# Rows spilled from full expert blocks: from blocks of 96 rows to units of 32 rows

## The reference

```python
g_sel = argmax(x @ w_group + b_group)            # one of 4 groups
top_v, top_i = top_k(le[rows, g_sel], 2)         # two of the 8 experts of that group
gate = softmax(top_v) * pg[rows, g_sel]
h = silu(xr @ w_gate[e]) * (xr @ w_up[e])        # 1024 -> 512
y[token] += gate * (h @ w_down[e])               # 512 -> 1024
```

## Time and profile before

| | us |
|---|---|
| median of three runs (1839.2, 1839.83, 1849.47) | 1839.83 |
| the profiled execution's own time | 1853.84 |
| its span | 1852.1 |
| PE busy (share of the span) | 1759.5 (95%) |
| DVE busy | 747.6 (40%) |
| ACT busy | 326.1 (18%) |
| POOL busy | 196.3 (11%) |
| mean granted TensorE clock | 0.975 |

### The profile page before, as it was taken

One profiled execution on the slowest core, in us unless ns is written; L12 is line 12 of the kernel. 1 busy time (PEld: TensorE's weight loads), 2 busy tenths in 40 slices (PEclk: granted clock), 3 DMA queues, 4 the chain that ended last, 5 costly groups with the idle time before them and its releaser, 6 DMA issues. The chain is left out here.

```text
span 1852.1 us, 34664 instructions
## 1 busy us (share of the span) xinstructions
PE 1759.5 (95%) x15263; PEld 1143.8 (62%) x15263; DVE 747.6 (40%) x1172; ACT 326.1 (18%) x741; POOL 196.3 (11%) x190
## 2 busy tenths in 40 slices
PE   8999999999999999999989999759999999999976
PEld 4565556646666644445666665438777777778742
DVE  1213456515766743400013444554334443344337
ACT  1211224401334210110001111001011110011016
POOL 2100000002322000000000000041111111111103
PEclk9999999999999999999999999779999999999998
DMA  6261011001002041343110001529999999999967
GB/s 212 71 211 46 1 45 50 1 1 49 1 13 91 4 159 34 123 142 114 46 46 12 24 23 68 228 92 406 422 424 418 415 422 419 419 420 413 368 235 276
DMA packets 72887, 322.32 MB, mean 174 GB/s; under 512 B 14481, under 2 KB 29129, under 8 KB 59745
## 3 DMA queue, kind: packets, MB, share of 16 engines
q1 hardware_dynamic: 47856, 280.70, 38.0%
q10 hardware_dynamic: 17360, 22.03, 3.6%
q0 software_dynamic: 7584, 18.38, 2.8%
HBM read 288.05 MB, written 37.65 MB: 176 GB/s over the span
## 5 line engine op out<-in xcount | busy, mean ns | idle before, releaser
L860 PE MATMUL psum<-arena 128*32 128x256 f32 x6144 | 375.0, 381 | 14.3 <-DVE arena L1942 6.3
L860 PEld LDWEIGHTS psum<-arena 128*32 128x32 f32 x6144 | 270.3, 110 | 108.5 <-issue 53.3
L457 PE MATMUL psum<-arena 128*128 128x512 f32 x640 | 282.7, 600 | 3.0 <-issue 3.0
L1466 DVE COPY arena<-psum 128x512 f32<-128x512 f32 (+6 forms) x128 | 83.8, 663 | 369.1 <-PE psum L457 201.3
L457 PEld LDWEIGHTS psum<-arena 128*128 128x128 f32 x640 | 121.8, 193 | 150.5 <-issue 150.1
L869 PE MATMUL psum<-arena 128*32 128x256 f32 x3072 | 180.6, 379 | 0.7 <-DVE arena L1916 0.5
L680 PE MATMUL psum<-arena 128*128 128x352 f32 x576 | 177.9, 460 | 0.0
L442 PE MATMUL psum<-arena 128*128 128x352 f32 x576 | 170.8, 459 | 0.1
L869 PEld LDWEIGHTS psum<-arena 128*32 128x32 f32 x3072 | 139.2, 110 | 31.7 <-issue 1.4
L1174 ACT ACTIVATE arena<-psum 128x128 f32<-128x128 f32 (+7 forms) x193 | 94.1, 497 | 345.0 <-PE psum L435 244.0
L442 PEld LDWEIGHTS psum<-arena 128*128 128x128 f32 x576 | 109.4, 190 | 61.3 <-issue 0.8
(11 more groups left out here) (273 smaller groups left out, 1575.7 us busy)
## 6 DMA issues: line engine op xcount, KB each, us to landing
arena<-in_moe_w_down SPq DMA_DIRECT2D x34, 2048.0 KB, 15.2
arena<-in_moe_w_gate SPq DMA_DIRECT2D x34, 2048.0 KB, 13.2
arena<-in_moe_w_up SPq DMA_DIRECT2D x34, 2048.0 KB, 18.4
y_blocks<-arena ACTq DMA_DIRECT2D x136, 96.0 KB, 12.0
arena<-in_w_in SPq DMA_DIRECT2D x6, 2048.0 KB, 9.9
y_blocks<-arena ACTq DMA_DIRECT2D x1, 8448.0 KB, 45.9
arena<-in_x_prompt SPq DMA_DIRECT2D x9, 512.0 KB, 3.3
arena<-in_w_out SPq DMA_DIRECT2D x2, 2048.0 KB, 7.9
```

The lines of the kernel that those rows point to most:

```text
L457: last = mm(ps[0:n, c * 512:(c + 1) * 512], lhs(k), rhs(k)[:, c * 512:(c + 1) * 512], start=(k == 0), stop=(k == KD - 1))
L860: last = mm(out, xeT[:, b, a, k, :], gu[b][:, :, k, j * P:(j + 1) * P], start=(k == 0), stop=(k == KD - 1))
L1466: take(V.tensor_copy(out, src), key)
```

## The change

Rows of rank 96 and above are now worked in units of 32 rows. A unit has one gather, one gate column and one store of its own; it loads the three weights of its expert as a block did. `NU` = 66 units are possible, and every loop and every list of tests goes to that number. The number of units of an expert is its rows over 96, divided by 32 and rounded up; the units lie one after the other in the same space of `y_blocks`, three to a former block. The table `over_i` is larger (66 units by 32 experts), and it is worked out behind `tables_ready` and the gates, under a semaphore of its own (`over_ready`) for which all engines wait ahead of `n_over`. POOL writes six of the nine tiles of the second choice's `pick`, DVE the other three. A unit's buffer in PSUM is two banks apart from the other's, for gate and up as for down.

```diff
-            link(TS(ovn, cnt, 1.0 / C, -(C / 2 + 0.5) / C, ALU.mult, ALU.add))
+            link(TS(ovn, cnt, 1.0 / 32, 0.5 - 1.0 / 64 - NS, ALU.mult, ALU.add))
...
-            STT(RR, TB_, -float(C), RR, ALU.mult, ALU.add).then_inc(places_ready, 1)
-            link(TS(TA, TB_, 1.0, None, ALU.is_ge))
-            link(TT(OO, OO, TB_, ALU.add))
-            link(STT(OO, OO, float(NE - 1), EE, ALU.add, ALU.subtract))
+            link(STT(RR, TB_, -32.0, RR, ALU.mult, ALU.add))
+            link(TS(TA, TB_, float(NS), None, ALU.is_ge))
+            link(STT(OO, OO, float(NS * NE - NS), EE, ALU.add, ALU.subtract))
             link(TT(OO, OO, TA, ALU.mult))
-            link(TT(EE, EE, OO, ALU.add))
+            link(TT(TB_, EE, TB_, ALU.add))
+            link(TT(TB_, TB_, OO, ALU.add))
+            link(TS(EE, TB_, 1.0 / NS, -1.0 / NS, ALU.mult, ALU.add))
+            link(TS(EE, EE, ROUND, -ROUND, ALU.add, ALU.add))
+            link(STT(OO, EE, -float(NS), TB_, ALU.mult, ALU.add))
+            STT(RR, OO, 32.0, RR, ALU.mult, ALU.add).then_inc(places_ready, 1)
...
+                if k == 1:
+                    for t0, t1 in ((BY_POOL, NT - 1), (NT - 1, NT)):
+                        n, nt = rows_of(t0), t1 - t0
+                        last = TT(pick[0:n, 1, t0:t1, :], row_iota[0:n, :].unsqueeze(1).to_broadcast([n, nt, C]),
+                                  vals[0:n, 6, t0:t1].unsqueeze(2).to_broadcast([n, nt, C]), ALU.is_equal)
...
-            link(TT(over3, oend.unsqueeze(1).to_broadcast([P, NOVER, NE]),
-                    blk_iota[:, 0:NOVER].unsqueeze(2).to_broadcast([P, NOVER, NE]), ALU.is_le))
...
             take(V.tensor_copy(gates, both[:, 1]), ("GT",))
             emptied(dve, ("GT",))
+            link(TT(over3, oend.unsqueeze(1).to_broadcast([P, NU, NE]),
+                    unit_iota.unsqueeze(2).to_broadcast([P, NU, NE]), ALU.is_le))
+            link(V.tensor_reduce(over_f[:, 0:NU], over3, AX.X, ALU.add))
+            link(TS(over_f[:, 0:NU], over_f[:, 0:NU], float(NE - 1), None, ALU.min))
+            link(V.tensor_copy(over_f[:, NU:NU + 1], oend[:, NE - 1:NE]))
+            V.tensor_copy(over_i, over_f).then_inc(over_ready, 1)
```

PE, SP and ACT in `spilled` (DVE has the silu of one tile in place of three):

```diff
-                for a in range(NS):
-                    for k in range(KD):
...
+                for k in range(KD):
+                    for q in range(4):
+                        last = mm(O_U[b][32 * q:32 * q + 32].rearrange("p (m n) -> p m n", m=2), xeT[:, b, 0, k, :],
+                                  gu[b][:, :, k, q * P:(q + 1) * P], start=(k == 0), stop=(k == KD - 1))
+                last.then_inc(o_gu, 1)
...
             with pe.If(n_over > 2):
-                with pe.Fori(1, NOVER // 2) as i:
+                with pe.Fori(1, NU // 2) as i:
...
-                    sp.wait_ge(o_gu, 3 * j - 3)
+                    sp.wait_ge(o_gu, j - 1)
...
-                    sp.wait_ge(o_dn, 2 * j - 2)
+                    sp.wait_ge(o_dn, j - 1)
...
+                act.wait_ge(o_gu, j + 1)
+                A(sg[:, 0, :], O_U[b], ACT.Exp, scale=-1.0).then_inc(g_exp, 1)
                 act.wait_ge(o_gate, j + 1)
-                act.wait_ge(o_dn, 2 * j + 1)
+                act.wait_ge(o_dn, j + 1)
...
+                A(ye[b][:, 0, :], O_Y[b], ACT.Copy, scale=gate2[:, b, 0:1]).then_inc(o_y, 1)
                 act.wait_ge(o_y, j + 1)
-                store_y(y_dram[bass.ds(j * C + NE * C, C), :], b, o_out)
+                for q in range(4):
+                    act.dma_start(y_dram[bass.ds(j * 32 + NE * C, 32), 256 * q:256 * q + 256],
+                                  ye[b][32 * q:32 * q + 32, 0, :]).then_inc(o_out, 16)
                 act.wait_ge(o_out, 64 * j + 64)
                 A(lnv[:, 0:1], eps_ln, ACT.Copy)
...
             with act.If(n_over > 2):
-                with act.Fori(1, NOVER // 2) as i:
+                with act.Fori(1, NU // 2) as i:
...
-            for j in range(NOVER):
+            pool.wait_ge(over_ready, 1)
+            n_over = pool.value_load(over_i[0:1, NU:NU + 1], min_val=0, max_val=NU)
+            for j in range(NU):
                 with pool.If(n_over > j):
...
-                    gather(NE + j, j % 2, [o_x[j % 2]] * NS)
+                    gather_tile(NE + j // NS, j % 2, j % NS, 0, o_x[j % 2])
```

More of the change, by code:

```diff
@@ L30 @@
 NB = NE + NOVER
+NU = NS * NOVER
 ALPHA = 2.0 ** 0.25
@@ L227, in build @@
         assert rt[0] <= R + 17408
+        over3 = view(R + 13312, "j e", j=NU, e=NE)
+        gates_of_unit = gates.rearrange("p n a -> p (n a)")
         g1 = view(0, "t n", t=NT, n=D)
@@ L831, in _ @@
                 for t in range(NT):
-                    if k == 1:
+                    if k == 1 and t < BY_POOL:
                         pe.wait_ge(row_ready, t + 1)
@@ L899, in _ @@
             down(1).then_inc(y_done, 1)
-            pe.wait_ge(tables_ready, 1)
-            n_over = pe.value_load(over_i[0:1, NOVER:NOVER + 1], min_val=0, max_val=NOVER)
-            O_Y = psum[:, 6 * BANK:8 * BANK]
+            pe.wait_ge(over_ready, 1)
+            n_over = pe.value_load(over_i[0:1, NU:NU + 1], min_val=0, max_val=NU)
+            O_U = [psum[:, 2 * b * BANK:2 * b * BANK + 256] for b in range(2)]
+            O_Y = [psum[:, (4 + 2 * b) * BANK:(4 + 2 * b) * BANK + 256] for b in range(2)]
             def spilled(j, b, turn_n):
@@ L911, in spilled @@
                     pe.wait_ge(y_ready, NE - 1 + j)
-                for a in range(NS):
-                    for k in range(KD):
[L914 to L918, removed]
-                pe.wait_ge(o_down[b], 16 * turn_n + 16)
[L920 to L931, removed]
+                for k in range(KD):
[3 more added lines that the diff above has]
+                last.then_inc(o_gu, 1)
+                pe.wait_ge(o_down[b], 16 * turn_n + 16)
+                if not isinstance(j, int):
+                    pe.wait_ge(o_y, j - 1)
+                pe.wait_ge(o_h, j + 1)
+                for k in range(KE):
+                    for q in range(4):
+                        last = mm(O_Y[b][32 * q:32 * q + 32], hhT[:, b, 0, k, :], wd[b][:, k, q * 256:(q + 1) * 256],
+                                  start=(k == 0), stop=(k == KE - 1))
+                last.then_inc(o_dn, 1)
             with pe.If(n_over > 0):
@@ L1125, in _ @@
             load_down(NE - 1, 1, NE - 2)
-            sp.wait_ge(tables_ready, 1)
-            n_over = sp.value_load(over_i[0:1, NOVER:NOVER + 1], min_val=0, max_val=NOVER)
+            sp.wait_ge(over_ready, 1)
+            n_over = sp.value_load(over_i[0:1, NU:NU + 1], min_val=0, max_val=NU)
             def spilled(j, b):
@@ L1148, in _ @@
             with sp.If(n_over > 2):
-                with sp.Fori(1, NOVER // 2) as i:
+                with sp.Fori(1, NU // 2) as i:
                     for b in range(2):
@@ L1404, in _ @@
             y_rows(NE - 1, 1, 3, NE // 4 - 1)
-            act.wait_ge(tables_ready, 1)
-            n_over = act.value_load(over_i[0:1, NOVER:NOVER + 1], min_val=0, max_val=NOVER)
-            O_Y = psum[:, 6 * BANK:8 * BANK]
+            act.wait_ge(over_ready, 1)
+            n_over = act.value_load(over_i[0:1, NU:NU + 1], min_val=0, max_val=NU)
+            O_U = [psum[:, 2 * b * BANK:2 * b * BANK + P] for b in range(2)]
+            O_Y = [psum[:, (4 + 2 * b) * BANK:(4 + 2 * b) * BANK + 256] for b in range(2)]
             def spilled(j, b):
@@ L1798, in _ @@
                     V.memset(place[:, :, NT - 1, :], 0.0)
-                    V.memset(pick[:, 0, NT - 1, :], 0.0)
+                    V.memset(pick[:, :, NT - 1, :], 0.0)
                 if s >= 4:
@@ L1838, in _ @@
             of_chosen(e_iota, EE)
+            link(TS(EE, EE, float(NS), None, ALU.mult))
             rk = filled(dve, ("RK",))
@@ L1950, in _ @@
             dve_expert(NE - 1, 1, NE // 2 - 1, last_one=True)
-            n_over = dve.value_load(over_i[0:1, NOVER:NOVER + 1], min_val=0, max_val=NOVER)
+            dve.wait_ge(over_ready, 1)
+            n_over = dve.value_load(over_i[0:1, NU:NU + 1], min_val=0, max_val=NU)
             def spilled(j, b, turn_n):
-                dve.wait_ge(o_x[b], 16 * NS * turn_n + 16 * NS)
-                turn_x(b).then_inc(o_xt, 1)
+                dve.wait_ge(o_x[b], 16 * turn_n + 16)
+                V.transpose(xeT[:, b, 0], xe[:, b, 0].rearrange("p (d k) -> p k d", k=KD)).then_inc(o_xt, 1)
                 if isinstance(j, int):
@@ L1982, in _ @@
             with dve.If(n_over > 2):
-                with dve.Fori(1, NOVER // 2) as i:
+                with dve.Fori(1, NU // 2) as i:
                     for b in range(2):
@@ L2096, in _ @@
             pool.wait_ge(masks_ready, 1)
-            link(Q.memset(pick[:, 1, NT - 1, :], 0.0))
             pool.wait_ge(places_ready, 1)
-            for t in range(NT):
-                n = rows_of(t)
-                Q.tensor_scalar(pick[0:n, 1, t, :], row_iota[0:n, :], vals[0:n, 6, t:t + 1], None, ALU.is_equal)\
+            for t in range(BY_POOL):
```

(1 more changed line is left out.)

66 lines of the change are left out of this document (28 added, 38 removed).

## The result

The changed kernel takes **1888.09 us** (median of four runs, 1881.43 to 1892.24), the kernel before beside it on the same chip 1844.34: a ratio of **1.024, 95% interval 1.0201 to 1.0278**, slower by some 44 us. The forecast was 1875 us, with a range of 1856 to 1895 and a chance of 0.84 for slower by over 1%. The sign and the size came out. Of the three terms of the sum C came within 1 us, A within 1.2 us, and B has the wrong mechanism and lies outside its own bounds.

What follows compares the result with a forecast made beforehand. It took PE and the DMA engines as both full in the expert stage, so earlier delays carry through. Terms 2.6 + 11 + 21.5 + 0 gave +35 us, 1889 for the profiled execution, scaled to a 1875 us median; range 1856 to 1895.

Steps and rivals of the forecast that it cites:

- C: Loop behind unit 1: ACT's 31 idle iterations of failed tests stand uncovered ahead of `fin_ready`, 0.68 us each, +21.5 us.
- A: Routing ahead of the first expert: extra small DVE instructions and the larger table of experts delay the first transpose, +2.6 us.
- B: Spilled units up to the last store's landing: a third weight set paces unit 2, +11 us, bounds +6 and +14.
- ACT's wait for each store doesn't decide: Spilled units: stores land in about 9 us under a full queue, about when the next exponential is ready.
- The low clock: PE in the spilled units: idle gaps keep the granted clock at 1.2 GHz, 0.104 us a pass.
- the terms 2.8 and 3.6: Unit 2 behind its up landing: 2.8 us for silu and 3.6 us for down's 32 passes, within 18.0 us.
- the weights already set the pace: Spilled blocks before the change: PE's start on block 1 at 1780.34 matched up's landing within 0.1 us.
- D: Empty loops on SP, DVE, POOL and PE are covered before the last stage: 0, up to 5 us.
- Hidden tests: Rival: sequencers run the empty iterations ahead during waits for weights or store; +13.6 us, 1853 us; chance 0.09.
- two units: Rival: only two units are made and the loop isn't entered; -1 us, 1839 us; chance 0.03.
- a code fetch at every jump: Rival: one jump per idle iteration on ACT or PE costs 3.37 us; some +140 us, 1980 us; chance 0.06.
- Units do not wait for weights: Rival: third weight set lands in time, ACT paces units at 10.4 us each; +22 us, 1862 us; chance 0.08.

Runs made afterwards that it cites:

- before_again: The kernel before the change, unaltered, run again for a second profile: 1848.4 us, ratio 1.0024; its profiled execution took 1839.58 us.
- table_late: Changed kernel with the units' table of experts computed behind the three transposes of expert 0's rows instead of ahead of them: 1889.17 us, ratio 1.0255.
- deferred: Changed kernel with ACT's wait for the stores of units 0 and 1 moved behind the last unit: 1873.84 us, ratio 1.0156.
- shared_set: Changed kernel with one set of weights fewer, unit 1 multiplying by unit 0's weights as both have the same expert: 1872.98 us, ratio 1.0172.
- all_four: Changed kernel with loop cut to two iterations, store waits moved back, table behind the first transposes, and one weight set fewer: 1859.93 us, ratio 1.0078.

## Why the prediction was right, and where it was not

*A, routing, +2.6: measured 3.5 to the first transpose (1230.42 against 1226.88), 3.8 to expert 0's exponential against before_again, 0.4 of it ahead of the edits.* The extra small instructions cost about what was said: PE's table product starts at 1215.98, 0.9 us later than in the earlier trace rows, for 1.05. Two things were missed. The product also lasts 6.22 us for 5.08: the granted clock was 0.67 over its last third, where in before_again it was 0.86 over the second half. And the first gather's issue on POOL took 2.77 us beside DVE's two long instructions, 1.26 us in before_again and in table_late, where DVE is free; in table_late a later issue, beside the moved table, took 2.37. In the timeline of the changed kernel:

```profile
1215.98 6.22 PE L838 MATMUL psum<-arena 128*96 128x108 f32 x36 [12.41 <-DVE arena L1879]
...
1225.11 2.36 DVE L1902 TENSOR_TENSOR arena<-arena 128x2112 f32<-128x2112 f32 x1
1225.84 2.77 POOL L2119 DMA_INDIRECT arena<-x_rows,consts  x1 [8.42 <-DVE consts L1898]
1227.50 2.35 DVE L1904 TENSOR_REDUCE arena<-arena 128x66 f32<-128x2112 f32 x1
...
1230.42 0.63 DVE L1950 STREAM_TRANSPOSE arena<-arena 128x256 f32<-128x256 f32 x1
```

The table's 2.36 and 2.35 us are the 2.4 that was taken, and the transpose follows without idle time, as said. The slower issue was named, as the ground of the upper bound of 5 us. The 3.8 us were carried through the experts (3.8 at expert 31's exponential), as the forecast took every delay ahead of the first expert to be; but the 1.6 us that table_late won there were lost by then.

*B, the units, +11: measured +18.1 (+20.9 against the first profile). The mechanism was wrong, and both figures lie outside the bounds of +6 and +14.* The step that failed is "ACT's wait for each store doesn't decide", with "about 9" us for a store under a full queue. Its row held four stores near 1745 and was scaled by packets; but unit 0's store was not slow by its size, it landed only behind the loads that were queued. With a third set of weights issued at 1754.64 to 1766.34 on SP's queue and the experts' stores ahead of it on ACT's own, unit 0's store landed 21.8 us after the copy, when the queue was empty. The wait then put units 1 and 2 one behind the other at 10.05 and 10.45 us, where the forecast had unit 1 under cover. In numbers: without the wait the stretch is 58.0 (deferred), +6.9, near the forecast's lower bound of +6; ACT's wait adds 11.1. The third set (13.9 us at the store, shared_set) and the wait overlap. That taking out either gives the same 58.0 is chance, since shared_set also pays PE's long jump. The low clock was right for the downs (3.59 us for 32 passes, 0.112 each, at a granted clock of 0.52), not for unit 2's gate and up, which ran 64 passes in 3.66 us right behind a down, at 1.00. Two smaller things in the working: the terms 2.8 and 3.6 stand 0.2 and 0.3 us above what its own rows give (2.6, and 32 x 0.104 = 3.3). And "the weights already set the pace" rests on a near tie: PE was at block 0's down until 1780.09, and in before_again it went from that down to block 1 without idle time, 2.8 us after up had landed (1763.2). At that point PE set the pace.

*C, the tests that fail, +21.5: measured 21.0, of which 20.7 are new.* From ACT's sequencer after the change (durations in ns, first and last start):

```profile
L1435 ACTq ALU_OP  x32: 35/35/35, 1809.4 to 1829.8; - x32
```

31 steps in 20.4 us, 0.66 us each; 0.68 was worked out. POOL's list of failed tests gave nearly the right price. The estimate by the 108 ns of the Trainium skill (Advanced Engine Details and Errata, Control Flow Timing) was 16.6; the trace decides for its own rows.

*D, other engines' loops, 0: right.* In the timeline PE's L949 is released by the gathers:

```profile
1839.33 2.93 PE L949 MATMUL psum<-arena,consts 128*128 128x512 f32 x3 [33.95 <-DMA arena<-y_blocks,consts]
```

It comes 9.2 us after L1441, where the forecast counted 9.6. PE's loop took 1.11 us an iteration, for the forecast's 1.0 to 1.1, and ended at 1838, so the cover was "just enough", as said; none of its branches took more than 0.36 us.

*The rivals.* Hidden tests, two units and a code fetch at every jump are out by the counts and by C. "Units do not wait for weights" was half right without its price: they wait for a store instead, so its 10.4 us a unit hold (10.05 and 10.45), but from 1788.8 on, in this execution, and not from 1768.6. The rule of Runtime: NRT & Kernel Launch, Instruction fetch mechanics (the Trainium skill), that a taken branch to code outside the fetched window waits, did not bear on the loop; PE's 6.85 us over the general path in shared_set agrees with it, though no run shows what that time went into.

*The total.* The sum was +35 on an execution whose expert stage was 12 us longer than usual, scaled to 1875. Against the like execution the terms are 3.8 + 18.1 + 20.7 - 0.8 = 41.8, so 1839.83 + 41.8 = 1881.6, the lower end of what was measured. The largest miss is B's 7 us; A's 1.2 more, C's 0.8 less and 0.8 less elsewhere make up the rest of 41.8 for 35. That the total lies in the range is luck as far as B goes: the range was wide for the price of an iteration, not for B.

## What to carry to other kernels

A loop over a dynamic count that runs to its largest value costs its failed tests on the engine that releases the next stage, 0.66 us an iteration on ACT here; look also at the loop of the engine that is wanted next, 1.11 us on PE and hidden by 1 us. End such a loop near the count, with the rest behind one test (in all_four 1.8 us from the last store to the release). An in-order wait for a store cost not the store but the loads that were still queued: price it at the time when the queue runs empty, and put the wait where the buffer is next needed. And pieces that are cut finer should not load the same weights again: a third set took 14 us of a full queue here, and the PE time that the smaller passes saved went into waiting.

## What the runs showed of the hardware that was not expected

Beside a saturated stream of weights the stores of 96 KB take 27 us to land (median; in an empty queue 1.9 to 3.6 us, and 1.5 to 1.6 us for a unit's 32 KB), without slowing the experts. The lag shows at the end of the stream: in three runs the first spilled store landed 2 to 3 us behind the last load. Issues can also hold the engine that makes them: the four issues of expert 31's store took 6.66 us on ACT, where the four before them took 2.14 and a unit's in the empty queue 1.74, and ACT's exponential of unit 0, whose input PE had finished at 1754.5, started at 1759.90; why those four were slow is not shown. One taken jump on PE over the general path took 6.85 us in two kernels, while a branch in ACT's loop took 0.04 to 0.06 us and a whole iteration with its three branches 0.66 us.
